# Gated one-hot selectors of a scatter: from three VectorE operations a unit to sixteen ScalarE operations and one on VectorE

## The reference, cut to what matters

```python
s = jnp.einsum('thpd,hpnd->thpn', q, keys)                 # two lists of 128 scores for each of 8 heads
sv, si = lax.top_k(s, 16)
cv, ci = lax.top_k(sums of the two lists, 16)
e = i1 * 128 + i2                                          # expert number, i1 and i2 in 0..127
gate = jax.nn.softmax(cv, axis=-1)
act = gelu(einsum('td,thkd->thk', xb, u_tab[e]))
y = einsum('thkd weighted by gate * act', v_tab[e])
```

## Time and profile before

| | |
|---|---|
| median of 3 runs | 4015.3 us (4001.01 to 4023.02) |
| span of the profiled execution | 3988.8 us |
| mean granted clock of TensorE | 0.983 |
| scatter of unit 0 to scatter of unit 39, layer 1 | 921.83 to 1383.56 us |
| the same, layer 2 | 2897.56 to 3360.09 us |

### The profile page before, as it was taken

How to read it: one execution, slowest core, us unless ns; L and a number is a source line. 1 busy time by engine, 2 the same in 40 slices (tenths; PEclk the granted TensorE clock), 3 DMA queues, 4 the chain that set the end, 5 groups by cost and what they waited for, 6 DMA issues and landing times.

```text
span 3988.8 us, 59456 instructions
## 1 busy us (share of the span) xinstructions
PE 3877.4 (97%) x23204; PEld 3461.4 (87%) x23204; DVE 2869.6 (72%) x4841; ACT 1540.6 (39%) x2349; POOL 2259.3 (57%) x1452
## 2 busy tenths in 40 slices
PE   8999999999999999999999999999999999999999
PEld 6778599999999999999477876999999999999994
DVE  5764368955887878888567552799458887798885
ACT  1443145553333334444314432555532333343343
POOL 0032069887777657668101310888877774688861
PEclk9988999999999999999999899999999999999999
DMA  4201146666899999999221021566679899999992
GB/s 122 52 13 48 43 170 215 214 233 218 305 322 320 316 361 388 395 395 343 78 66 39 12 75 43 188 214 210 220 246 312 304 322 333 346 383 380 378 340 71
DMA packets 417975, 900.99 MB, mean 226 GB/s; under 512 B 94496, under 2 KB 242208, under 8 KB 416032
## 3 DMA queue, kind: packets, MB, share of 16 engines
q1 hardware_dynamic: 272288, 552.91, 40.2%
q0 software_dynamic: 90112, 268.76, 18.7%
q10 hardware_dynamic: 55296, 75.52, 5.2%
HBM read 773.87 MB, written 123.15 MB: 225 GB/s over the span
## 4 chain that ended last, share of the span: by engine, by line
PE 52%; POOL 15%; DMA 14%; DVE 11%; issue 5%; ACT 2%; SPq 0%; DVEq 0%; ACTq 0%; POOLq 0%
PE banks L1364 11%; PE banks L826 7%; PE banks L1376 7%; POOL peer_gates L2079 6%; PE banks L1438 5%; DMA u_stage<-peer_ut 5%; POOL u_stage L2095 4%; PE banks L1473 4%; DMA gated<-dense_gelus 3%; PE banks L1275 3%; POOL u_stage L2087 3%; DMA peer_gates<-peer_v,u_stage 3%; PE banks L1293 3%; DVE normed L2729 2%; DMA normed<-peer_ut 1%
## 5 line engine op out<-in xcount | busy, mean ns | idle before, releaser
L2079 POOL DMA_INDIRECT peer_gates<-peer_v,u_stage x512 | 733.8, 1433 | 387.3 <-DVE normed L2729 157.6
L1438 PE MATMUL banks<-gated_parts,v_parts 128*128 128x320 f32 x6144 | 911.1, 310 | 19.9 <-DVE gated_parts L2776 18.2
L1438 PEld LDWEIGHTS banks<-gated_parts,v_parts 128*128 128x128 f32 x6144 | 905.8, 189 | 25.4 <-issue 25.2
L1364 PE MATMUL banks<-peer_x_parts,u_parts 128*128 128x448 f32 x3168 | 664.0, 367 | 3.3 <-DVE u_parts L2715 3.3
L1364 PEld LDWEIGHTS banks<-peer_x_parts,u_parts 128*128 128x128 f32 x3168 | 590.5, 188 | 49.6 <-DVE u_parts L2715 4.1
L2095 POOL DMA_INDIRECT u_stage<-dense_gelus,u_stage x256 | 374.5, 1463 | 106.9 <-issue 77.4
L1364 PE MATMUL banks<-peer_x_parts,low_s 128*128 128x448 f32 x1696 | 398.3, 367 | 0.5 <-DVE low_s L2715 0.5
L2729 DVE SCALAR_TENSOR_TENSOR normed<-peer_gates,u_stage,normed 128x1024 f32<-128x1024 f32 x254 | 327.5, 1289 | 85.3 <-DMA peer_gates<-peer_v,u_stage 71.0
L2745 DVE SCALAR_TENSOR_TENSOR peer_gates<-peer_gates,u_stage 128x1024 f32<-128x1024 f32 x254 | 325.4, 1281 | 81.3 <-DMA peer_gates<-peer_v,u_stage 71.3
L1869 ACT ACTIVATE u_stage<-banks 128x448 f32<-128x448 f32 x256 | 139.2, 544 | 621.8 <-PE banks L1364 616.8
L2087 POOL DMA_INDIRECT u_stage<-gelus,u_stage x256 | 329.0, 1285 | 78.1 <-issue 78.0
(11 more groups left out here) (355 smaller groups left out, 6642.6 us busy)
## 6 DMA issues: line engine op xcount, KB each, us to landing
v_stage<-peer_v SPq DMA_DIRECT2D x256, 512.0 KB, 7.7
u_stage<-peer_ut SPq DMA_DIRECT2D x244, 512.0 KB, 5.2
dense_gelus<-u_stage ACTq DMA_DIRECT2D x256, 224.0 KB, 5.3
gates<-peer_gates SPq DMA_DIRECT2D x16, 2560.0 KB, 20.3
u_stage<-gates SPq DMA_DIRECT2D x64, 640.0 KB, 8.9
gated<-dense_gelus SPq DMA_DIRECT2D x256, 160.0 KB, 7.6
x<-peer_ut SPq DMA_DIRECT2D x64, 512.0 KB, 4.7
u_raw<-peer_ut SPq DMA_DIRECT2D x64, 512.0 KB, 4.9
```

Of the source, the lines that this page charges most:

```text
L1364: ins = mm(PS[:, d % 2, 0:DW], u_part(n, a, k), XR[:, b, k, DENSE0:TOK], start=(k == 0 and m == 0), stop=(k == KT - 1 and m == 2))
L1438: ins = mm(vc[k][:, 0:PW3], VR[:, s, b, k * 128:(k + 1) * 128], HR[:, s, a, :], start=(j == 0 and m == 0), stop=(j == NKEYS - 1 and m == 2))
L2079: eng.indirect_dma_start(out=GU[:, t % 4, :], out_offset=None, in_=din["peer_v"].rearrange("l i j d -> (l i j) d"), in_offset=bass.Indirec ...
```

## The change

The other selector, `OH2`, stays one VectorE comparison for 8 tokens at once. `OH1` was made of two VectorE operations (compare with iota, multiply by the gate), each over 128 x 1024. It is now made by ScalarE token by token: 8 times (iota - i1) squared, then 8 times ReLU(gate - 2 x square), each over 128 x 128 with a pointer to one column of `IT` as bias. Where n equals i1 the square is 0 and the gate is left; elsewhere the square is at least 1 and the gate at most 1, so ReLU gives 0. For the bias i1 is stored negated: the copy into `IT` is split into one with scale -1 and one of the other two planes. ACT makes units 0 and 1 after its two `high_u` calls and before its loop over units; in the loop it makes unit u + 2 between the copies and the dense rows of unit u. PE's scatter waits for a second semaphore, `oh_gated`.

```diff
-                    act.did(A(IT[:, :, COL[i] - DENSE0:...], b[:, 0:3, 0:ACROSS[i]], ACT.Copy).then_inc(act_done, 1), "drained", "it", L, i)
+                    act.did(A(IT[:, 0, cols], b[:, 0, 0:ACROSS[i]], ACT.Copy, scale=-1.0).then_inc(act_done, 1))
+                    act.did(A(IT[:, 1:3, cols], b[:, 1:3, 0:ACROSS[i]], ACT.Copy).then_inc(act_done, 1), "drained", "it", L, i)
...
                 pe.wait_ge(oh_ready, n + 1)
+                pe.wait_ge(oh_gated, n + 1)
...
+            def gated_one_hots(u):
+                n = UNITS * L + u
+                if u >= 2:
+                    act.wait_ge(scattered, 2 * n - 2)
+                for t in range(8):
+                    c = 8 * u + t
+                    ins = A(OH1[:, u % 2, t, :], const("iota"), ACT.Square, bias=IT[:, 0, c:c + 1])
+                ins.then_inc(oh_squared, 1)
+                act.wait_ge(oh_squared, n + 1)
+                for t in range(8):
+                    c = 8 * u + t
+                    ins = A(OH1[:, u % 2, t, :], OH1[:, u % 2, t, :], ACT.Relu, scale=-2.0, bias=IT[:, 2, c:c + 1])
+                ins.then_inc(oh_gated, 1)
+
+            for i in SPREAD:
+                act.wait_ge(act_done, at("drained", "it", L, i))
+            pair_done(act, L, PAIRS - 4)
+            gated_one_hots(0)
+            gated_one_hots(1)
             for u in range(UNITS):
...
+                if u + 2 < UNITS:
+                    gated_one_hots(u + 2)
                 for q in rows_of_unit(u):
                     later_row(q)
...
-                it = lambda c: bc(IT[:, c, 8 * u:8 * u + 8], 2, 128)
-                TT(OH1[:, u % 2], bc(const("iota"), 1, 8), it(0), ALU.is_equal).then_inc(oh_chosen, 1)
-                TT(OH2[:, u % 2], bc(const("iota"), 1, 8), it(1), ALU.is_equal)
-                dve.wait_ge(oh_chosen, n + 1)
-                TT(OH1[:, u % 2], OH1[:, u % 2], it(2), ALU.mult).then_inc(oh_ready, 1)
+                TT(OH2[:, u % 2], bc(const("iota"), 1, 8), bc(IT[:, 1, 8 * u:8 * u + 8], 2, 128), ALU.is_equal).then_inc(oh_ready, 1)
```

More of the change, by code:

```diff
@@ L502, in trunk @@
     d_gate = [sem(f"gates_stored{i}") for i in range(2)]
-    oh_chosen, oh_ready, scattered, gates_copied = sem("oh_chosen"), sem("oh_ready"), sem("scattered"), sem("gates_copied")
+    oh_squared, oh_gated, oh_ready, scattered, gates_copied = sem("oh_squared"), sem("oh_gated"), sem("oh_ready"), sem("scattered"), sem("gates_copied")
     d_v = [sem(f"v_loaded{i}") for i in range(NVB)]
@@ L1911, in _ @@
                     b = bank("it", L, i).rearrange("p (c r) -> p c r", c=4)
-                    act.did(A(IT[:, :, COL[i] - DENSE0:COL[i] - DENSE0 + ACROSS[i]], b[:, 0:3, 0:ACROSS[i]], ACT.Copy).then_inc(act_done, 1), "drained", "it", L, i)
+                    cols = slice(COL[i] - DENSE0, COL[i] - DENSE0 + ACROSS[i])
+                    act.did(A(IT[:, 0, cols], b[:, 0, 0:ACROSS[i]], ACT.Copy, scale=-1.0).then_inc(act_done, 1))
+                    act.did(A(IT[:, 1:3, cols], b[:, 1:3, 0:ACROSS[i]], ACT.Copy).then_inc(act_done, 1), "drained", "it", L, i)
                 if pos + 2 < NT:
```

## The result

The changed kernel took 4069.9 us (median of 4 runs, 4045.07 to 4081.04) where the kernel before took 4019.2 us beside it (4001.01 to 4024.37): a ratio of 1.0135, 95% interval 1.0101 to 1.017. I had forecast 4013 us, and 4038 us as the upper end. It is slower by some 54 us (1.35% of 4015.3), and the likeliest case of the prediction was wrong.

The account below looks back on a forecast made before the run. PE was taken to bound the scatter stretches. A 21.6 us start loss less a 24 us gain gave -2.4 us against the 4015.3 us median, so 4013 us, range 3995 to 4038 us.

Parts of the forecast that it names:

- the likeliest case of the prediction: Gain in the scatter loop and loss at its start nearly cancel: 4013 us, own range 4003 to 4030, chance 0.66.
- Gain, 24 us of 27.2: Scatter stretches: PE lost 27.2 us over the units of both layers; earlier DVE selectors would win back 24 us.
- Start, 17.8 + 3.8: Ahead of scatter 0 in both layers: PE waits 17.8 us for ACT's selectors and loses 3.8 us to the lower clock.
- The cost of a set: ACT's selectors: eight 128x128 operations take 2.44 us, a unit 5.0 us; ACT's busy time rises by 390 us.
- ReLU brought no table load: Rival on ACT: ReLU needs another table than Gelu, two loads per unit, 4082 us; chance 0.04.
- DVE 182 us less: Selectors on DVE: two operations fewer per unit, 2.27 us each unit, 182 us of DVE time over 80 units.
- The rival that ACT becomes late: After late loads, PE waits for the gelu behind ACT's sixteen operations; about 4050 us, chance 0.20.
- The rival that more comes back: Lateness fully gone, no clock lost at the start, V stretch waits for DVE shrink; 3996 us, chance 0.10.
- Small ones: Split copy into `IT`, below 0.5 us per operation beside PE's work, and POOL's gathers waiting for `oh_ready`: both priced at nothing.
- Where they lie in the steady state: Scatter loop: first gelu slips 0.9 us behind ACT's new operations, DVE has 2.27 us more room; priced at nothing.

Follow-up runs that it names:

- Experiment 9: Changed kernel, with POOL doing two 128x512 subtractions into scratch ahead of the 9th, 17th and 25th gathers of its run; ratio 0.9993 to the kernel before.
- experiment 10: Changed kernel, with POOL doing two 128x512 subtractions into scratch ahead of the 17th gather alone; ratio 1.0007 to the kernel before.
- experiment 3: Changed kernel, with DVE making both selectors of units 0 and 1 and ACT's starting from unit 2; ratio 0.9938, repeated 0.9939.
- 7: Changed kernel, with POOL's first gather waiting for DVE's selector of unit 2; ratio 1.0083 to the kernel before.
- 2: Changed kernel, with POOL's first gather waiting for DVE's selector of unit 3; ratio 1.0079 to the kernel before.
- experiment 5: Changed kernel, with 28 extra 128x512 comparisons into scratch on DVE ahead of its loop; ratio 1.0009 to the kernel before.
- experiment 6: Changed kernel, with DVE making both selectors of units 0 and 1, then waiting until unit 1 is scattered; ratio 1.0015 to the kernel before.
- experiment 8: Kernel before, with DVE's selectors of units 0 and 1 behind ACT's high parts and DVE then silent until unit 1 is scattered; ratio 1.0208.
- 11: Changed kernel, with POOL doing two 128x512 subtractions into scratch ahead of the first gather of its run; ratio 1.0124 to the kernel before.
- 1: Kernel before, with DVE's selectors of units 0 and 1 moved behind ACT's high parts; ratio 1.0049.
- 4: Kernel before, with sixteen more ACT operations per unit, from unit 2 on, into scratch that nobody reads; ratio 1.0031.
- the 128x4 break: Changed kernel, with POOL doing one 128x4 subtraction, waited for, ahead of the 17th gather; ratio 1.0118 to the kernel before.
- the met wait: Changed kernel, with POOL waiting ahead of the 17th gather for a semaphore already counted, doing no work there; ratio 1.0109 to the kernel before.

## Why the prediction was wrong

**The sum held, and one term was missing.** Experiment 9 is the changed kernel without the slow stretch. It gives 0.9993 (0.9972 to 1.0014); my 4013 over 4015.3 is 0.9994. That the two agree so closely is luck, as the interval is 17 us wide and experiment 10 gave 1.0007; the terms are better judged one by one in its trace.

- *Gain, 24 us of 27.2.* In experiment 9 the 39 units took 451.1 and 452.0 us, of which 2.6 and 2.0 are unit 0 behind the start wait. What is left of the old loss is 0 and 1.5 us; in experiment 3 it is 0.1 and 0. The term was right, a little low.
- *Start, 17.8 + 3.8.* 8.97 + 8.71 = 17.7 us, and unit 0 took 2.1 and 3.0 us over its pace, at a granted clock of 0.50 in its first 3.7 us in both layers. Right for the wait, 1.3 us low for the clock.
- *The cost of a set.* Eight operations took 2.44 and 2.45 us, as in the earlier trace rows. The groups add up to 392 us over both layers. Right; ACT's busy time as a whole rose by 366.2 of the 390 forecast, since the records overlap their neighbours' (the copies end at 937.79, the squares behind them begin at 937.69). ReLU brought no table load: 101 before, 101 after, and none in either scatter stretch. That is as the Trainium skill has it (ScalarE: Activation LUTs, Table sets: the hidden batching unit).
- *DVE 182 us less.* 181.3.
- *The rival that ACT becomes late.* Refuted. No late load of the loop made PE wait for a gelu. It had the right sign and nearly the time ("about 4050", where its own terms add up to 4057), by a wrong mechanism.
- *The rival that more comes back.* Nothing bears it out. PE's waits for DVE in the V stretch, 18.2 us before, were 30.9 in the kernel after and 30.9 in experiment 9. In the other runs' traces they lie between 11.6 and 38.4 us, so one trace of each doesn't tell what the change did to them.

**The step that failed** is under *Small ones*: "POOL's gathers wait for `oh_ready` of unit 0, now 2.27 us earlier, but for the last natural store as well: nothing". I looked only at when the gathers start. What that "nothing" stood for measured 28.0 and 28.1 us. The change also took away what DVE did among the gathers: two of its three selector operations, and, since scatter 0 came 9 us later, the ones of unit 2 and the low parts that would have begun at 930. From 926.7 on DVE was silent while POOL issued gather after gather, and some 13 us later ACT and DVE were held and PE's matmuls crawled. "So: nothing" for DVE's room (*Where they lie in the steady state*) was right for the loop and wrong for its start.

**What the runs show of the cause.** POOL's run of gathers is needed: with nothing changed but POOL's stream the stretch moves (7) or goes (2, 9, 10). It must go on for long without a break of some 2 us of its own. DVE's work in it counts: filled in, it put the stretch off (5), and taken away, it brought the stretch into versions that had none (6, 8). But how much of it is enough isn't known, as some of it did not help in 7 and did in 3. Not needed are ACT's sixteens (8) or a stop of PE (6, 7), and the added code alone doesn't take it away (11). A stop of PE without a silent DVE isn't enough (1), nor ACT's load (4). Since ACT's semaphores, DVE's and PE's issue are all late at once, it seems that something that they share is held up by the run; that is a conclusion from the traces and not tested.

**What stays open.** Which resource that is. No run tells either whether the recording has a part in it: each timed execution here comes with a span and a granted clock, so none is known to have run unrecorded. And how a break works ahead of its time: up to its pause experiment 10 has the same instructions as the changed kernel, but ACT was in time 12.7 us after the first gather, when the pause at the 17th was still 7 us off, and scatter 1 ran at full speed at 951.4, 16.3 us after it. So it seems that not the gathers gone by decide, but something about those that stand behind. A queue on POOL that fills would fit the places of the pauses, but not the 128x4 break or the met wait, unless a break must last as well; this is argued and not shown.

**Beside it.** I took the profiled execution's time as the median, 26.5 us above its span. It was not: the profiled execution after took 4071.76 us with a span of 4070.0. So 1.8 us lie around a span, and the profile before was of an execution near 3991 us (an estimate, 3988.8 + 1.8), faster than all four timed ones. The terms are differences, and so the forecast did not suffer.

## What to carry to other kernels

Where an edit takes work off an engine, look also at the work that this one did between other engines' transfers: here operations that were "hidden" stood among POOL's gathers, and without them 28 us a layer were lost, more than the edit won. Look with suspicion at a long run of indirect DMAs (32 here, 40 us) in a stretch in which the other engines are waiting for each other's semaphores; here two small operations of POOL ahead of the 17th element gather took all of it away. And price the first pass of a moved step by itself: the way to 0.994 was to leave the first two units with DVE, or, with the run of gathers broken up, to give ACT unit 0 in a wait that it had anyway.

## What the runs showed of the hardware

- During such a run of gathers PE issued single matmuls 0.7 us apart or a multiple of it (1.4, 2.1, 2.8; kernel after), with one gap of 12 us (experiment 8), at a DMA share as low as 0.02 (kernel after, 946 to 953) and 0.05 (experiment 6, 965 to 970). They began between 13 and 31 us after the first gather of the run, or, where DVE's filler or a pause came first, 37 to 38 us after it.
- For a dense row that PE had finished at 941, ACT, free from 942.6 on, began its gelu at 952.4; in experiment 8 ACT's two copies of one scatter, done at 953.8, began at 960.3 and 971.6.
- Undisturbed gathers took 0.94 us each with a pitch of 1.25 (kernel after); beside 128x512 comparisons of DVE 1.15 (experiment 5); beside its 128x1024 ones up to 1.97 (kernel before).
